# Regrouping the first loads of a two-layer decoder trunk on one core, and loading ScalarE's root table before x arrives

## The reference

```python
for l in range(DEPTH):
    h = rmsnorm(x, pre_mix_g[l])
    z = h @ w_in[l]                     # q | k | v | u | g, 2560 columns
    ...
    attn = dilated_mixture_attention(q, k, v)
    rec = gelu(g) * rg_lru(causal_dwconv(u, conv_w[l], conv_b[l]), ...)
    mixed = concat(rmsnorm(attn), rmsnorm(rec))
    x = x + rmsnorm(mixed @ w_out[l], post_mix_g[l])
    h = rmsnorm(x, pre_ffn_g[l])
    f = swiglu(h, ...) if l % 2 == 0 else moe_ffn(h, ...)
    x = x + rmsnorm(f, post_ffn_g[l])
```

## Time and profile before

| | us |
|---|---|
| median of three runs | 1459.18 (1459.09 to 1459.87) |
| the profiled execution | 1459.41 |
| its span, first to last instruction | 1457.6 |
| TensorE busy in the span | 1439.0 (99%) |
| VectorE busy | 1196.2 (82%) |
| ScalarE busy | 1032.0 (71%) |
| DMA, mean | 312 GB/s |

### The profile page before, as it was taken

How to read it: one execution, slowest core, us unless ns; L and a number is a source line. 1 busy time by engine, 2 the same in 40 slices (tenths; PEclk the granted TensorE clock), 3 DMA queues, 4 the chain that set the end, 5 groups by cost and what they waited for, 6 DMA issues and landing times.

```text
span 1457.6 us, 20750 instructions
## 1 busy us (share of the span) xinstructions
PE 1439.0 (99%) x7076; PEld 1193.5 (82%) x7076; DVE 1196.2 (82%) x1378; ACT 1032.0 (71%) x1258; POOL 14.5 (1%) x13
## 2 busy tenths in 40 slices
PE   8999999999999999999999999999999999999997
PEld 7887888888887688888888888888888888888885
DVE  7867656555776798898899899989889889989997
ACT  7665445445565677787797787788778779778774
POOL 0000000000000200000000000000000000001000
PEclk9999999999999999999999999999999999999999
DMA  9525874554433399999999999999999999999991
GB/s 367 208 100 197 339 274 177 201 200 173 147 143 127 112 423 409 361 393 388 378 370 397 375 362 409 376 353 400 386 358 399 388 366 378 397 373 372 420 400 65
DMA packets 68611, 454.11 MB, mean 312 GB/s; under 512 B 9424, under 2 KB 9552, under 8 KB 16592
## 3 DMA queue, kind: packets, MB, share of 16 engines
q1 hardware_dynamic: 60768, 432.47, 76.6%
q10 hardware_dynamic: 6640, 16.78, 3.2%
q0 software_dynamic: 1152, 4.19, 0.7%
HBM read 438.21 MB, written 15.20 MB: 311 GB/s over the span
## 4 chain that ended last, share of the span: by engine, by line
PE 94%; DVE 3%; ACT 2%; issue 1%; DMA 0%; DVEq 0%; ACTq 0%
PE psum L472 26%; PE psum L474 26%; PE psum L473 26%; PE psum L760 7%; PE psum L763 4%; PE psum L822 2%; ACT lru_b L938 1%; PE psum L479 1%; DVE hn L1300 1%; DVE xs L1322 1%; DVE hn L1316 1%; PE psum L621 0%; PE psum L561 0%; PE psum L805 0%; PE psum L499 0%
## 5 line engine op out<-in xcount | busy, mean ns | idle before, releaser
L1211 DVE TENSOR_TENSOR w_lo<-ring,w_hi 128x1024 fp32r<-128x1024 f32 x812 | 941.0, 1219 | 57.1 <-ACT w_hi L925 56.4
L925 ACT ACTIVATE w_hi<-ring 128x1024 fp32r<-128x1024 f32 x812 | 807.5, 1053 | 56.1 <-PE psum L474 49.7
L472 PE MATMUL psum<-w_hi,hT_both 128*128 128x512 f32 (+1 forms) x1088 | 424.4, 390 | 1.4 <-DVE hT_both L1222 1.4
L474 PE MATMUL psum<-w_hi,hT_both 128*128 128x512 f32 (+1 forms) x1088 | 417.6, 384 | 0.0
L473 PE MATMUL psum<-w_lo,hT_both 128*128 128x512 f32 (+1 forms) x1088 | 416.8, 383 | 0.0
L474 PEld LDWEIGHTS psum<-w_hi,hT_both 128*128 128x128 f32 x1088 | 204.4, 188 | 41.1
L472 PEld LDWEIGHTS psum<-w_hi,hT_both 128*128 128x128 f32 x1088 | 204.6, 188 | 40.7 <-DVE hT_both L1222 1.8
L473 PEld LDWEIGHTS psum<-w_lo,hT_both 128*128 128x128 f32 x1088 | 204.8, 188 | 38.4 <-issue 0.2
L472 PE MATMUL psum<-w_hi,act_hi 128*128 128x512 f32 x560 | 218.9, 391 | 0.9 <-DVE act_lo L1222 0.9
L474 PE MATMUL psum<-w_hi,act_lo 128*128 128x512 f32 x560 | 218.2, 390 | 0.0
L473 PE MATMUL psum<-w_lo,act_hi 128*128 128x512 f32 x560 | 218.2, 390 | 0.0
(11 more groups left out here) (236 smaller groups left out, 898.5 us busy)
## 6 DMA issues: line engine op xcount, KB each, us to landing
ring<-moe_gate SPq DMA_DIRECT2D x112, 1024.0 KB, 7.2
ring<-moe_up SPq DMA_DIRECT2D x112, 1024.0 KB, 7.6
ring<-moe_down SPq DMA_DIRECT2D x112, 1024.0 KB, 7.3
ring<-in_units SPq DMA_DIRECT2D x20, 1024.0 KB, 7.9
ring<-dense_gate SPq DMA_DIRECT2D x14, 1024.0 KB, 4.9
ring<-dense_up SPq DMA_DIRECT2D x14, 1024.0 KB, 4.8
ring<-dense_down SPq DMA_DIRECT2D x14, 1024.0 KB, 4.8
ring<-out_units SPq DMA_DIRECT2D x8, 1024.0 KB, 5.4
```

The source lines that it names most:

```text
L472: pe.matmul(dst, s_hi, m_hi, start=start, stop=False)
L474: return pe.matmul(dst, s_lo, m_hi, start=False, stop=stop)
L925: act.activation(w_hi[:, h % AHEAD, :], ring[:, n % RING, (h % 2) * HCOLS:(h % 2 + 1) * HCOLS], ACT.Copy).then_inc(hi_ready, 1)
L1211: dve.tensor_tensor(w_lo[:, h % AHEAD, :], ring[:, (h // 2) % RING, (h % 2) * HCOLS:(h % 2 + 1) * HCOLS], w_hi[:, h % AHEAD, :].bitcast(F3 ...
```

## The change

`con` is loaded in two parts, the identity (128 columns) right behind `gain` with a semaphore of its own, and the rest later. `par` and the rest of `con` are moved behind unit 0. Unit 0 is loaded in two halves with a semaphore each, and ScalarE waits for the first half ahead of h0 and for the second ahead of h1. `load_sqrt` is called once at the start of ScalarE's work, ahead of the wait for x. TensorE waits for the identity alone, and issues two more fillers between the transposes of tile 0 and those of tile 1.

```diff
+        ident_loaded = sem("ident_loaded")
         consts_loaded = sem("consts_loaded")
+        first_half_loaded = sem("first_half_loaded")
...
-            sync.dma_start(con[:, :], consts).then_inc(consts_loaded, 16)
-            sync.dma_start(par[:, :], params).then_inc(params_loaded, 16)
+            sync.dma_start(con[:, 0:P], consts[:, 0:P]).then_inc(ident_loaded, 16)
...
-                sync.dma_start(ring[:, n % RING, :], src).then_inc(unit_loaded[n % RING], 16)
+                if n == 0:
+                    sync.dma_start(ring[:, 0, 0:HCOLS], src[:, 0:HCOLS]).then_inc(first_half_loaded, 16)
+                    sync.dma_start(ring[:, 0, HCOLS:UCOLS], src[:, HCOLS:UCOLS]).then_inc(unit_loaded[0], 16)
+                    sync.dma_start(par[:, :], params).then_inc(params_loaded, 16)
+                    sync.dma_start(con[:, P:NCON], consts[:, P:NCON]).then_inc(consts_loaded, 16)
+                else:
+                    sync.dma_start(ring[:, n % RING, :], src).then_inc(unit_loaded[n % RING], 16)
...
-                    pe.wait_ge(consts_loaded, 16)
+                    pe.wait_ge(ident_loaded, 16)
                 else:
                     warm(3, 6)
                 turn_rows_of(n, 0)
-                if n > 0:
-                    warm(4, 7)
+                warm(4 if n > 0 else 2, 7)
                 turn_rows_of(n, 1)
...
-                if h % 2 == 0:
+                if h == 0:
+                    act.wait_ge(first_half_loaded, 16)
+                elif h == 1 or h % 2 == 0:
                     act.wait_ge(unit_loaded[n % RING], loaded)
...
             act.wait_ge(cleared, 1)
+            load_sqrt()
+
             def mixer(layer):
```

## The result

| | before | after |
|---|---|---|
| median of 11 runs, us | 1459.15 (1458.95 to 1459.87) | 1461.85 (1460.59 to 1464.29) |
| ratio, 95% interval | | 1.002 (1.0012 to 1.0028) |
| profiled execution, us | 1459.41 | 1464.29 |
| its span | 1457.6 | 1462.4 |

The change makes the kernel 2.7 us slower, by 0.19%, just inside the 0.2% that the prediction called "same"; but the interval lies clear of no change, and 1457.6 with its range of 1456.9 to 1459.3 was wrong, in its sign too. The spread of the runs grew from 0.9 to 3.7 us.

What follows compares the result with a forecast made beforehand. TensorE, busy in 99% of the span, was taken as the bound. Early table, `gain` wait and full-clock fillers moved the stream's start from 15.51 to 13.97; 1459.18 − 1.54 = 1457.64 us, range 1456.9 to 1459.3.

Steps and rivals of the forecast that it cites:

- The second Square: ScalarE, first stage: no table load before it, so one early load serves Square and root; roots 2.59 us earlier.
- `gain` did take over as the bound: VectorE's first reciprocal would wait for `gain` until 7.51, so 1.14 of the 2.59 us come through.
- the identity and the first half were in time: First loads: identity at 7.9 to 8.4, hidden before 8.60; unit 0's first half at 9.2, wanted at 10.36.
- fillers, transposes and end fillers: TensorE, first stage: at full clock, tile 1's transposes start at 11.37 and the matmul stream at 13.97, against 15.51.
- The margin of 0.17 at h2: VectorE's `w_lo` of h2 done at 19.54, wanted at 19.71; this caps the gain at about 1.6 to 1.7 us.
- Unit 0 in halves: Load step: halves land at 9.2 and 10.4, keeping the table saving whole; later loads slip 0.2 to 0.3 us, covered.
- whatever lets the long stream of matmuls begin earlier should take the end along: Whole kernel: TensorE is busy in 99% of the span, so only the first real matmul's start counts.
- The last paragraph of the prediction: Signs to check; wrong if the stream starts at 14 and the end doesn't follow, a later stage being bound elsewhere.
- B: First stage: the clock falls again at 11.36; 1459.2, or 1460.0 if it rises late; chance 0.12.
- C: Later norm stages, unchanged: the clock falls in shifted idle gaps, up to 1.7 us each, 1461.1 at two; chance 0.05.
- D: ScalarE: the compiler still loads a table ahead of Square; stream at about 16.6, 1460.3; chance 0.03.
- The term that was put too high: Stream start 1.54 us earlier than in the profiled execution, taken off the median whole.

Runs made afterwards that it cites:

- e1: The changed kernel with the two gate-block transfers issued early, in ScalarE's idle time behind the roots of x: 1457.71 us.
- e3: The changed kernel with SP waiting for both gate blocks before it issues unit 10 of the ring: 1459.12 us.
- e7: The changed kernel without the early root table and the fillers between the tiles, so the regrouped loads alone: 1459.37 us.
- e9: The changed kernel with the gate blocks issued early and without the two fillers between the tiles: 1457.50 us.
- e8: The changed kernel with the gate blocks stored whole with their zeros, in 4 KB pieces instead of 256 bytes: 1458.18 us.
- e4: The changed kernel with three fillers (six passes) ahead of TensorE's wait for the gate blocks in the first layer: 1461.14 us.

## Why the prediction was wrong

*Right, by its steps.* The second Square did show that one table serves both. `gain` did take over as the bound (7.28 against 7.51), the identity and the first half were in time, the clock stayed full, and fillers, transposes and end fillers summed to 13.97 against 13.75. TensorE's lead at the gates was 1.76 against 1.54. The margin of 0.17 at h2 held. e1 gives the forecast's time, 1457.71.

*The step that failed* is in "Unit 0 in halves": "`small_functions` behind it moves by 0.3 and is wanted later too". Behind `small_functions` the program has `load_layer`, with the two transfers of the blocks (in the trace they are issued right behind h6, at 19.49, ahead of the first row of `small_functions` at 19.85); I followed ScalarE's computing behind h6 and not its DMA issues. Their 16.8 us to landing stood in the trace of before, and 37.1 against 38.54 is a margin of 1.4 us, smaller than the 1.54 that the sum takes off TensorE's side. So "whatever lets the long stream of matmuls begin earlier should take the end along" fails 23 us behind the stream's start: the lead of 1.76 became a wait of 3.39, and 2.99 for the clock on top. The last paragraph of the prediction names the case, that the stream starts at 14 and the end doesn't follow, and then no chance was given to it. The second miss would have come behind the first: a sum in which the blocks still land at 37.1 is too kind. By e3, overtaking costs only what was gained, and the larger part, 2.7 us, comes from the ring's next unit, which an earlier TensorE issues earlier.

*The rivals.* B, the clock falling at 11.36 again, didn't happen in the profile of the changed kernel. C, the clock falling in a place that the change doesn't touch, had the right kind of price: the fall at 39.26 cost 3 us in the profiled execution. But its cause was named wrong. It wasn't a known gap at a shifted time but a new gap of over 3 us. D is excluded by the single table load. The slower side got 0.02 beyond 0.2%, and the range ended at 1459.3, because every rival but C was looked for inside the stage that the change edits.

*The term that was put too high.* The forecast took off 1.54 us from the median, though part of it was the clock's fall in the profiled execution. In the profile of e7, whose first stage is that of before up to the loads, there is no fall. The third weight load of the stream, in the kernel before and in e7:

```profile
15.63 0.19 PEld L474 LDWEIGHTS psum<-hT_both,w_lo 128*128 128x128 f32 x1
...
15.11 0.19 PEld L481 LDWEIGHTS psum<-hT_both,w_lo 128*128 128x128 f32 x1
```

It comes 0.52 earlier. The executions of before lie mostly in two groups, 1459.0 to 1459.3 and 1459.4 to 1459.9, which are probably those without and with this fall; the profiled one is of the second, but only 0.23 above the median. So some 0.3 of the 1.54 should not have come off the median. It came out near all the same (1.48 in e1), since the stream after began 0.2 to 0.3 earlier than forecast: errors that offset each other, which is luck.

## What to carry to other kernels

When a tuned stretch is shortened, list every transfer that lands between the edit and the next hard wait, with its landing and the time at which its first reader gets there; a margin smaller than the gain decides the result, and an issue that hangs on another transfer doesn't move with the engines. A transfer in small pieces, on a second queue beside a stream of large ones, lives from the stream's pauses, and whatever makes the consumer faster also closes them. Issue it early (e1) and the change brings 1.5 us, 1.6 without its fillers (e9); make its pieces large instead (e8) and it brings 0.9.

## What the runs showed of the hardware

- Two queues on the same DMA engines alternate packet by packet, with 256 bytes as with 4 KB beside 8 KB: 102 packets of q10 beside 100 of q1 in 2 us before, 48 beside 49 in e8. So the two transfers of 128 KB took 16 to 20 us each, and with twice the bytes in 4 KB pieces 8 to 10.
- Three microseconds without matmuls at 37 to 40 us cost another 3 in the profiled execution, for the clock stayed at 1.2 GHz from 39.26 to 46.08; with six filler passes in the wait it was 2.4 throughout (e4). Idle 2.16 us ahead of the transposes kept the full clock in e7, where 2.40 lost it in the earlier trace rows; the Trainium skill (TensorE: Matmul & The Clock Gate, What's actually happening) says that the point of change varies from run to run. The profiles of these two kernels, with nearly the same first stage, agree; no kernel here has two profiles.
- A table load was followed by its activation within 0.01 us (1.18 + 1.28 = 2.46, start 2.47), again without the drain that the Trainium skill (ScalarE: Activation LUTs, What ACT_TABLE_LOAD costs) adds to each load.
